# Eight modulation blocks instead of ten ahead of the first GEMM, each in a buffer of its own and loaded by one DMA

## Chip, cores and metric

The kernel runs on one core of one Trainium2 chip. The metric is the device time of one execution in microseconds (us), the median over several runs. One execution was also recorded by the hardware profiler; all rows below come from it. The engines are TensorE (PE for matmuls, PEld for weight loads), VectorE (DVE), ScalarE (ACT), GpSimd (POOL) and SyncE (SP), which issues the large DMAs.

## What is computed

Two transformer-like blocks follow each other on 256 latent tokens of width 1024; the first block also carries 256 context tokens. Here only the start matters. Nine modulation vectors per layer come from the conditioning vectors `c` and `c_ctx`, and shift, scale and gate what follows:

```python
def modulate(x, gain, shift, scale):
    return rms_norm(x, gain) * (1 + scale) + shift

def swiglu(h, w_in, w_out):
    a, b = jnp.split(h @ w_in, 2, axis=-1)
    return (jax.nn.silu(a) * b) @ w_out
# w_mod: (2 layers, 1024, 9 * 1024), applied to silu(c) and silu(c_ctx); b_mod is added
```

The first thing that the first block does is a SwiGLU on the modulated norm of x, which needs the shift and the scale of the first norm of layer 0, that is the first 2 × 1024 columns of `w_mod`.

## The kernel before

**Modulation blocks.** `w_mod` is taken in 72 blocks of 256 columns and 1024 rows (1 MB each, two tiles of 128 columns). A block goes through four engines. SP loads it as f32 (`mod_load`, L476 to L483): two DMAs of 512 KB, one for each tile, into `M32[k]`, where k alternates between two buffers. A tile's run in HBM is 128 floats, 512 bytes. ACT writes the f16 high part `MWH[k]` (`mod_split`, L954, in the helper `copy`, L944). DVE writes the f16 rest `MWL[k]` (`mod_split`, L1316, its instruction is L1319). PE multiplies both parts with silu(c) (`pe_mod`, L560, its matmuls are L568 and L569), and DVE drains the eight columns (`mod_drain`, L1321, L1325).

**What holds the blocks back.** SP may load a tile again when DVE has split the one before in that buffer (`mod_lo`). ACT may split a block when PE has used the one two before (`mod_used`). PE may start a block when the one two before is drained (`mod_drained`).

**The order at the start.** SP issues x and ctx, small rows, then the loads of the ten blocks of `MOD_FIRST`, then the first pair of weight blocks of the GEMM `ffn_0a_in` (four DMAs into `W32`, L487), then two modulation loads for that GEMM, then in a loop weights and modulation loads by turns. Each engine is one queue in program order, SP too. DVE splits a pair of blocks and then drains the pair before. After the tenth block come `mod_finish`, which adds the bias and makes the norm's gain, a small matmul for the relative bias (L749, L1574), three of four weight splits (L1313), and `dve_apply` of norm 0 (L1469, L1475) with ACT's half of it (L1060). Only then do both engines split the GEMM's first modulation blocks (`begin_mods`). On PE, block 0 of `ffn_0a_in` (`one`, L612, matmuls L608 to L610) starts chunk by chunk as norm 0 is applied. After it comes one modulation block, after weight block 1 another, and so on (`turn_of`, L646).

**POOL.** When the ten early blocks are used (`mod_used`, L1734), POOL issues the mask and 32 small-run loads `in_na_rpb` (L1743), and when they have landed it multiplies and adds on them (L1746, L1749). The result is used from the fourth GEMM on.

**The arena.** One SBUF tensor, `arena`, holds most of this at hand-set offsets: `M32` from 19968 on, `MWH` and `MWL` from 24064 on. Norm 0's squares take 0 to 4096, and `onehot` and `rel_mask` 8704 to 9728.

Of the kernel before, what the change touches and what calls it, by code (L numbers as in the profile page):

```python
# [21 lines left out]
ALU = mybir.AluOpType  # L22
# [4 lines left out]
P = 128  # L27
D = 1024
DC = D // P
# [16 lines left out]
W_SCALE = 64.0  # L46
# [85 lines left out]
def program(nc, io, out):  # L132
    ctx = ExitStack()
    with ctx:
# [3 lines left out]
        def sem(name):  # L138
            return ctx.enter_context(nc.semaphore(name))
# [46 lines left out]
        GH, GL = area(0, FC, BOTH, dt=F16), area(FC * SEQ, FC, BOTH, dt=F16)  # L186
        ffn_s, ffn_g = area(2 * FC * SEQ, 2, BOTH), area(2 * FC * SEQ + 1024, 2, BOTH)

        M32 = [area(19968 + 2048 * k, 2, DC, P) for k in range(2)]
        MWH = [area(24064 + 2048 * k, 2, DC, P, dt=F16) for k in range(2)]  # L190
        MWL = [area(25088 + 2048 * k, 2, DC, P, dt=F16) for k in range(2)]

# [36 lines left out]


        loaded = [[sem(f"loaded_{k}{t}") for t in range(2)] for k in range(2)]
        mod_loaded = [[sem(f"mod_loaded_{k}{t}") for t in range(2)] for k in range(2)]
        mod_hi, mod_lo = sem("mod_hi"), sem("mod_lo")
        mod_used, mod_drained = sem("mod_used"), sem("mod_drained")
        hi_ready = sem("hi_ready")
# [136 lines left out]


        MOD_BLOCKS = N_MOD * DC
        MOD_FIRST = 10
        m = MOD_FIRST
        for name, pairs in (("ffn_0a_in", FC // 2), ("ffn_0b_in", FC // 2), ("ffn_1a_in", 9)):
            g = next(x for x in GEMMS if x["name"] == name)
            g["mods"], g["m0"] = pairs, m
# [87 lines left out]
        @block.sync  # L467
        def _(sp):
            sp.dma_start(x_tok[0], io["x"][0].rearrange("(t p) d -> p t d", p=P)).then_inc(x_loaded, 16)
            sp.dma_start(x_tok[1], io["ctx"][0].rearrange("(t p) d -> p t d", p=P)).then_inc(x_loaded, 16)  # L470
            sp.wait_ge(rows_clear, 1)
            load_rows(sp, ROWS[:8])

            mod_w = io["w_mod"].rearrange("l (c p) n -> p l c n", p=P)

            def mod_load(m0, i, k):  # L476

                layer, first = divmod(m0, MOD_BLOCKS // 2)
                for t in range(2):
                    if not (isinstance(i, int) and m0 + 2 * i < 2):  # L480
                        sp.wait_ge(mod_lo, 2 * (m0 + k - 2) + t + 1 + 4 * i)
                    src = mod_w[:, layer, :, bass.ds(256 * (first + k) + P * t + 512 * i, P)]
                    sp.dma_start(M32[k][:, t], src).then_inc(mod_loaded[k][t], 16)  # L483

            def load(g, wv, k, t, col0, kp):
                src = wv[:, kp * g["kc"]:(kp + 1) * g["kc"], bass.ds(col0, P)]
                sp.dma_start(W32[:, k, t, 0:g["kc"], :], src).then_inc(loaded[k][t], 16)  # L487

            for g in GEMMS:
                wv = g["w"].rearrange("(c p) n -> p c n", p=P)  # L490

                def pair(i, slot_free, g=g, wv=wv):
                    for k in range(2):
                        for t in range(2):
                            slot_free(k, t)
                            if g["kind"] == "ffn":
                                load(g, wv, k, t, (2 * i + k) * P + t * FF, 0)
                            elif g["cols"] == 256:
                                load(g, wv, k, t, 512 * i + 256 * k + P * t, 0)
                            else:  # L500
                                load(g, wv, k, t, g["cols"][2 * i + k] + P * t, 0)

                def split_before(i, w0=g["w0"]):

                    return lambda k, t: sp.wait_ge(lo_ready, 2 * (w0 - 2 + k) + t + 1 + 4 * i)

                n, mods = g["blocks"] // 2, g["mods"]
                begin = 0
                if g["w0"] == 0:
                    for i in range(2):  # L510
                        for k in range(2):
                            mod_load(0, i, k)
                    with sp.Fori(2, MOD_FIRST // 2) as i:
                        for k in range(2):
                            mod_load(0, i, k)
                    pair(0, lambda k, t: None)
                    for k in range(2):
                        mod_load(g["m0"], 0, k)
                    begin = 1
                if mods:  # L520
                    if g["name"] == "ffn_0b_in":
                        pair(0, split_before(0))
                        sp.wait_ge(hy_lo, 4)
                        for k in range(2):
                            mod_load(g["m0"], 0, k)
                        begin = 1
# [12 lines left out]
                if g["parts"] == 2:  # L539
                    with sp.Fori(0, n // 2) as i:  # L540
                        for kp in range(2):
                            for k in range(2):
                                for t in range(2):
                                    split_before(2 * i + kp)(k, t)
                                    load(g, wv, k, t, 512 * i + 256 * k + P * t, kp)
                elif isinstance(g["cols"], list):
                    for i in range(n):
                        pair(i, split_before(i))
                elif begin < n:
                    with sp.Fori(begin, n) as i:  # L550
                        pair(i, split_before(i))

            sp.wait_ge(stored, 32)
# [3 lines left out]
        def _(pe):  # L557
# [43 lines left out]
            def pe_gemm(g, between={}):  # L601
# [44 lines left out]
                def turn_of(i, mods, first=False):  # L646
                    for b in range(2 * g["parts"]):
                        pair, kp = b // g["parts"], b % g["parts"]
                        one(b % 2, kp, pair, g["w0"] + b + 2 * g["parts"] * i, g["u0"] + pair + 2 * i, first and b == 0)
                        if mods:  # L650
                            pe_mod(g["m0"] + b + 2 * i, b)

# [289 lines left out]
        def _(act):  # L942
            def copy(dst, src, scale=1.0):
                return act.activation(dst, src, ACT.Copy, scale=scale)  # L944
# [6 lines left out]
                    act.wait_ge(loaded[k][t], 16 * (g["w0"] // 2 + 1) + 16 * i)  # L951
                    copy(WH[:, k, t, 0:g["kc"], :], W32[:, k, t, 0:g["kc"], :], W_SCALE).then_inc(hi_ready, 1)

            def mod_split(m0, i, k, first=False):  # L954

                if not first:
                    act.wait_ge(mod_used, m0 + k - 1 + 2 * i)
                for t in range(2):
                    act.wait_ge(mod_loaded[k][t], 16 * (m0 // 2 + 1) + 16 * i)
                    copy(MWH[k][:, t], M32[k][:, t], W_SCALE).then_inc(mod_hi, 1)  # L960

            def begin(g, ks=(0, 1)):
                for k in ks:
                    split(g, 0, k, True)

            def begin_mods(g):
                if g["mods"]:
                    for k in range(2):
                        mod_split(g["m0"], 0, k)
# [130 lines left out]
                act.activation(silu_c[:, :, s], pcol[:, at:at + DC], ACT.Silu).then_inc(silu_c_ready, 1)  # L1100
            act.wait_ge(silu_c_ready, 2)
            copy(silu_s[:, :, 0:2], silu_c[:, :, :]).then_inc(silu_hi, 1)
            for k in range(2):
                mod_split(0, 0, k, True)
            act_root(0)

            act.wait_ge(lg_abs, 1)
            act.activation(lgt[:, 1, :], lgt[:, 0, :], ACT.Exp, scale=-1.0).then_inc(lg_exp, 1)
            act.wait_ge(lg_u, 1)
            act.activation(lgt[:, 3, :], lgt[:, 2, :], ACT.Ln).then_inc(lg_ln, 1)  # L1110
            for i in range(1, MOD_FIRST // 2):
                for k in range(2):
                    mod_split(0, i, k)
            begin(GEMMS[0])

            def filter_step(n):
# [176 lines left out]
        def _(dve):  # L1293
# [15 lines left out]
            def split(g, i, k, tiles=(0, 1)):  # L1309

                for t in tiles:
                    dve.wait_ge(hi_ready, 2 * (g["w0"] + k) + t + 1 + 4 * i)
                    stt(WL[:, k, t, 0:g["kc"], :], W32[:, k, t, 0:g["kc"], :], W_SCALE, WH[:, k, t, 0:g["kc"], :],  # L1313
                        ALU.mult, ALU.subtract).then_inc(lo_ready, 1)

            def mod_split(m0, i, k):  # L1316
                for t in range(2):
                    dve.wait_ge(mod_hi, 2 * (m0 + k) + t + 1 + 4 * i)
                    stt(MWL[k][:, t], M32[k][:, t], W_SCALE, MWH[k][:, t], ALU.mult, ALU.subtract).then_inc(mod_lo, 1)  # L1319

            def mod_drain(m0, i, k):  # L1321

# [24 lines left out]
                link(ins)  # L1347

            def begin_mods(g):
                if g["mods"]:  # L1350
                    for k in range(2):
                        mod_split(g["m0"], 0, k)

# [194 lines left out]
            dve.wait_ge(silu_hi, 1)  # L1548
            tt(silu_s[:, :, 2:4], silu_c[:, :, :], silu_s[:, :, 0:2], ALU.subtract).then_inc(silu_s_ready, 1)
            dve_inverse(0)  # L1550
            for k in range(2):
                mod_split(0, 0, k)

            dve.wait_ge(lg_loaded, 32)
            stt(lgt[:, 0, :], lg[:, :], -1.0, lg[:, :], ALU.mult, ALU.max).then_inc(lg_abs, 1)
# [10 lines left out]
            for i in range(MOD_FIRST // 2):  # L1566
                if i + 1 < MOD_FIRST // 2:
                    for k in range(2):
                        mod_split(0, i + 1, k)
                for k in range(2):  # L1570
                    mod_drain(0, i, k)
            mod_finish(0, MOD_FIRST, [(0, 0)], [], [])
# [261 lines left out]
```

## Time and profile before

| | us |
|---|---|
| median of 3 runs | 2709.05 (2706.67 to 2709.97) |
| span of the profiled execution | 2703.6 |
| PE matmuls busy | 2579.7 (95%) |
| DVE busy | 1359.1 (50%) |
| ACT busy | 1091.2 (40%) |
| POOL busy | 247.2 (9%) |

The times are those of whole executions, and the span is that of one execution's instructions. Starts in the rows are microseconds from the start of the span. A row's "idle before" names what the engine waited for last. A row of a helper line (L944) says by its tile names what it works on.

### The profile page before, as it was taken

How to read it: one execution, taken by the hardware profiler on the slowest of the kernel's cores; microseconds unless marked ns; L12 is line 12 of the kernel's file. 1: busy time of each engine (PE TensorE's matmuls, PEld its weight loads, DVE VectorE, ACT ScalarE, POOL GpSimd, SP SyncE). 2: the span in 40 equal slices, each digit the busy share in tenths (PEclk: the TensorE clock that was granted, in tenths of full speed). 3: DMA queues.
4: the chain of work that ended last, by engine and by line, in shares of the span. 5: the costliest groups of instructions: out<-in, count | busy, mean ns of one | idle time of the engine just before them, and what ended most of it. 6: DMA issues, size and time to landing. Idle time of an engine off the chain costs nothing.

```text
span 2703.6 us, 45490 instructions
## 1 busy us (share of the span) xinstructions
PE 2579.7 (95%) x17855; PEld 1695.6 (63%) x17855; DVE 1359.1 (50%) x1911; ACT 1091.2 (40%) x1610; POOL 247.2 (9%) x235
## 2 busy tenths in 40 slices
PE   3899999999999999999999899999999999999999
PEld 3444444455644444444444578788888878778888
DVE  5855443363465553365432543466655545255654
ACT  5544323243354442254333311445544443344553
POOL 1800001004010000100002100120010000010001
PEclk7999999999999999999999999999999998589999
DMA  8976632330066653366543332258756754044674
GB/s 236 235 196 187 173 94 71 94 94 1 16 173 186 187 166 106 108 179 186 162 143 96 96 105 81 79 147 235 217 162 200 217 147 125 1 125 138 173 213 129
DMA packets 732733, 383.74 MB, mean 142 GB/s; under 512 B 12059, under 2 KB 729216, under 8 KB 732488
## 3 DMA queue, kind: packets, MB, share of 16 engines
q1 hardware_dynamic: 728312, 369.27, 48.7%
q0 software_dynamic: 3728, 10.98, 1.7%
q8 instruction: 85, 1.39, 0.2%
q10 hardware_dynamic: 576, 1.83, 0.2%
q14 instruction: 32, 0.26, 0.0%
HBM read 380.96 MB, written 1.08 MB: 141 GB/s over the span
## 4 chain that ended last, share of the span: by engine, by line
PE 88%; DVE 5%; DMA 3%; ACT 2%; issue 1%; POOL 0%; SPq 0%; ACTq 0%; DVEq 0%; POOLq 0%
PE PS L608 23%; PE PS L610 23%; PE PS L609 23%; PE PS L691 2%; DMA arena<-in_w_mod 2%; PE PS L627 2%; PE PS L626 2%; PE PS L625 2%; PE PS L715 2%; PE PS L694 1%; DVE WL L1313 1%; PE PS L863 1%; PE PS L585 1%; DVE arena L1469 1%; ACT WH L944 1%; PE PS L705 1%
## 5 line engine op out<-in xcount | busy, mean ns | idle before, releaser
L608 PE MATMUL PS<-XH,WH 128*128 128x256 f16 (+1 forms) x2912 | 948.5, 326 | 34.6 <-DVE XL L1475 20.8
L609 PE MATMUL PS<-XL,WH 128*128 128x256 f16 (+1 forms) x2912 | 948.0, 326 | 0.0
L610 PE MATMUL PS<-XH,WL 128*128 128x256 f16 (+1 forms) x2912 | 947.7, 325 | 0.0
L944 ACT ACTIVATE WH<-W 128x1024 f16<-128x1024 f32 (+1 forms) x520 | 550.4, 1106 | 636.8 <-PE PS L610 519.0
L1313 DVE SCALAR_TENSOR_TENSOR WL<-W,WH 128x1024 f16<-128x1024 f32 (+1 forms) x520 | 664.8, 1318 | 276.0 <-ACT WH L944 276.0
L608 PEld LDWEIGHTS PS<-XH,WH 128*128 128x128 f16 x2912 | 287.7, 99 | 222.9 <-issue 35.4
L610 PEld LDWEIGHTS PS<-XH,WL 128*128 128x128 f16 x2912 | 288.2, 99 | 181.7 <-issue 4.6
L608 PE MATMUL PS<-arena,WH 128*128 128x256 f16 (+1 forms) x1248 | 396.4, 318 | 1.9 <-DVE WL L1313 1.9
L609 PE MATMUL PS<-arena,WH 128*128 128x256 f16 (+1 forms) x1248 | 396.4, 318 | 0.0
L610 PE MATMUL PS<-arena,WL 128*128 128x256 f16 (+1 forms) x1248 | 396.4, 318 | 0.0
L609 PEld LDWEIGHTS PS<-XL,WH 128*128 128x128 f16 x2912 | 288.1, 99 | 171.9 <-issue 4.0
L976 ACT ACTIVATE arena<-PS 128x512 f32<-128x512 f32 (+1 forms) x132 | 64.6, 489 | 552.7 <-PE PS L610 552.7
L1359 DVE SCALAR_TENSOR_TENSOR arena<-PS,arena 128x512 f32<-128x512 f32 (+1 forms) x132 | 73.6, 558 | 401.7 <-ACT arena L976 401.7
L944 ACT ACTIVATE arena<-arena 128x1024 f16<-128x1024 f32 (+4 forms) x300 | 216.3, 761 | 50.4 <-DMA arena<-in_w_mod 20.7
L1720 POOL TENSOR_TENSOR arena<-arena 128x256 f32<-128x256 f32 (+1 forms) x60 | 80.0, 1334 | 1367.3 <-ACT arena L1020 1363.4
L1319 DVE SCALAR_TENSOR_TENSOR arena<-arena 128x1024 f16<-128x1024 f32 x144 | 173.1, 1243 | 21.9 <-ACT arena L944 21.8
L608 PEld LDWEIGHTS PS<-arena,WH 128*128 128x128 f16 x1248 | 122.1, 98 | 74.2 <-issue 4.5
L610 PEld LDWEIGHTS PS<-arena,WL 128*128 128x128 f16 x1248 | 122.1, 98 | 70.5
L609 PEld LDWEIGHTS PS<-arena,WH 128*128 128x128 f16 x1248 | 122.1, 98 | 70.0 <-issue 0.3
L1374 DVE TENSOR_SCALAR arena<-PS 128x512 f32<-128x512 f32 (+2 forms) x52 | 48.7, 937 | 190.0 <-PE PS L610 116.6
L944 ACT ACTIVATE arena<-PS 128x256 f32<-128x256 f32 (+1 forms) x117 | 49.4, 435 | 164.7 <-PE PS L705 95.1
L1428 DVE SCALAR_TENSOR_TENSOR X<-PS,modT,X 128x256 f32<-128x256 f32 x80 | 34.1, 479 | 154.5 <-PE PS L610 154.5
(225 smaller groups left out, 2309.1 us busy)
## 6 DMA issues: line engine op xcount, KB each, us to landing
arena<-in_w_mod SPq DMA_DIRECT2D x144, 512.0 KB, 6.8
W<-in_ffn_a_in SPq DMA_DIRECT2D x88, 512.0 KB, 5.0
W<-in_ffn_b_in SPq DMA_DIRECT2D x88, 512.0 KB, 4.7
W<-in_w_ffn_gu SPq DMA_DIRECT2D x88, 512.0 KB, 4.1
W<-in_ret_in SPq DMA_DIRECT2D x48, 512.0 KB, 4.1
W<-in_ffn_a_out SPq DMA_DIRECT2D x32, 704.0 KB, 5.5
W<-in_ffn_b_out SPq DMA_DIRECT2D x32, 704.0 KB, 5.9
W<-in_w_ffn_down SPq DMA_DIRECT2D x32, 704.0 KB, 5.7
```

The source lines that it names most:

```text
L608: mm(dst, wh, xh, start=(kp == 0 and c == 0), stop=False, skip_group_check=True)
L609: mm(dst, wh, xl, start=False, stop=False, skip_group_check=True)
L610: return mm(dst, wl, xh, start=False, stop=(kp == g["parts"] - 1 and c == kc - 1), skip_group_check=True)
L625: mm(dst, xh, wh, start=(c == 0), stop=False)
L626: mm(dst, xh, wl, start=False, stop=False)
L627: ins = mm(dst, xl, wh, start=False, stop=(c == kc - 1))
L944: return act.activation(dst, src, ACT.Copy, scale=scale)
L976: act.activation(ffn_s[:, k, 0:T], PS[:, 2 * k, 0:T], ACT.Silu, scale=1.0 / W_SCALE).then_inc(silu_done, 1)
L1313: stt(WL[:, k, t, 0:g["kc"], :], W32[:, k, t, 0:g["kc"], :], W_SCALE, WH[:, k, t, 0:g["kc"], :], ALU.mult, ALU.subtract).then_inc(lo_ready, 1)
L1319: stt(MWL[k][:, t], M32[k][:, t], W_SCALE, MWH[k][:, t], ALU.mult, ALU.subtract).then_inc(mod_lo, 1)
L1359: stt(ffn_g[:, k, 0:T], PS[:, 2 * k + 1, 0:T], 1.0 / W_SCALE, ffn_s[:, k, 0:T], ALU.mult, ALU.mult)\
L1720: tt(N["sq"][:, 0, 0:N["T"]], N["sq"][:, 0, 0:N["T"]], N["sq"][:, c, 0:N["T"]], ALU.add).then_inc(added_up, 1)
```

## The change

Ahead of the first GEMM there are eight modulation blocks instead of ten. Each has a buffer of its own, `M32_first[m]`: six areas of the arena not used by then, and the two of `M32`. SP issues the eight loads without a wait, one DMA of 1 MB each, whose runs in HBM are 256 floats, 1 KB. Blocks 8 and 9 move into `ffn_0a_in`: PE takes them after its weight block 0 and before its own block 10. SP loads them after the first weight pair. ACT and DVE split them at the head of `begin_mods`, and DVE drains each ahead of the split of block 10 or 11. All later modulation loads are also one DMA with one wait for both tiles. ACT and DVE read a tile as `M32[k][:, :, P * t:P * t + P]`, eight runs of 128 floats.

```diff
-        M32 = [area(19968 + 2048 * k, 2, DC, P) for k in range(2)]
+        M32 = [area(19968 + 2048 * k, DC, 2 * P) for k in range(2)]
+        M32_first = [area(n, DC, 2 * P) for n in (4096, 6144, 9728, 11776, 13824, 15872)] + M32
...
-        MOD_FIRST = 10
-        m = MOD_FIRST
+        MOD_FIRST, MOD_EARLY = 8, 2
+        m = MOD_FIRST + MOD_EARLY
...
-                for t in range(2):
-                    if not (isinstance(i, int) and m0 + 2 * i < 2):
-                        sp.wait_ge(mod_lo, 2 * (m0 + k - 2) + t + 1 + 4 * i)
-                    src = mod_w[:, layer, :, bass.ds(256 * (first + k) + P * t + 512 * i, P)]
-                    sp.dma_start(M32[k][:, t], src).then_inc(mod_loaded[k][t], 16)
+                sp.wait_ge(mod_lo, 2 * (m0 + k - 2) + 2 + 4 * i)
+                src = mod_w[:, layer, :, bass.ds(256 * (first + k) + 512 * i, 2 * P)]
+                sp.dma_start(M32[k], src).then_inc(mod_loaded[k], 16)
...
-                    for i in range(2):
-                        for k in range(2):
-                            mod_load(0, i, k)
-                    with sp.Fori(2, MOD_FIRST // 2) as i:
-                        for k in range(2):
-                            mod_load(0, i, k)
+                    for m in range(MOD_FIRST):
+                        sp.dma_start(M32_first[m], mod_w[:, 0, :, 256 * m:256 * m + 256]).then_inc(mod_first_loaded[m], 16)
                     pair(0, lambda k, t: None)
+                    for k in range(2):
+                        mod_load(MOD_FIRST, 0, k)
                     for k in range(2):
                         mod_load(g["m0"], 0, k)
...
                         one(b % 2, kp, pair, g["w0"] + b + 2 * g["parts"] * i, g["u0"] + pair + 2 * i, first and b == 0)
+                        if first and b == 0 and g["w0"] == 0:
+                            for m in range(MOD_FIRST, MOD_FIRST + MOD_EARLY):
+                                pe_mod(m, m % 2)
                         if mods:
                             pe_mod(g["m0"] + b + 2 * i, b)
...
+            def mod_first_split(m):
+                if m >= 2:
+                    act.wait_ge(mod_used, m - 1)
+                act.wait_ge(mod_first_loaded[m], 16)
                 for t in range(2):
-                    act.wait_ge(mod_loaded[k][t], 16 * (m0 // 2 + 1) + 16 * i)
-                    copy(MWH[k][:, t], M32[k][:, t], W_SCALE).then_inc(mod_hi, 1)
+                    copy(MWH[m % 2][:, t], M32_first[m][:, :, P * t:P * t + P], W_SCALE).then_inc(mod_hi, 1)
...
             def begin_mods(g):
-                if g["mods"]:
+                if g["w0"] == 0:
+                    for k in range(2):
+                        mod_split(MOD_FIRST, 0, k)
+                    for k in range(2):
+                        mod_drain(MOD_FIRST, 0, k)
+                        mod_split(g["m0"], 0, k)
+                elif g["mods"]:
                     for k in range(2):
                         mod_split(g["m0"], 0, k)
```

## Rows read from the trace of the kernel before

**Rows 1.** Chain that ended last, 0 to 160 us: start, length, what

```profile
1.25 10.52 DMA XL<-in_ctx
...
31.23 6.21 DMA arena<-in_w_mod
...
68.21 27.58 DMA arena<-in_w_mod
...
98.68 1.22 DVE WL L1313
99.95 0.39 PE PS L608
```

**Rows 2.** Timeline of DVE, 20 to 125 us: start, length, instruction, count, idle before

```profile
26.64 4.56 DVE L1319 SCALAR_TENSOR_TENSOR arena<-arena 128x1024 f16<-128x1024 f32 x4
...
34.02 2.36 DVE L1319 SCALAR_TENSOR_TENSOR arena<-arena 128x1024 f16<-128x1024 f32 x2 [0.29 <-ACT arena L944]
...
39.69 0.23 DVE L1325 TENSOR_REDUCE modT<-PS 128x4 f32<-128x8 f32 x2
42.11 3.60 DVE L1319 SCALAR_TENSOR_TENSOR arena<-arena 128x1024 f16<-128x1024 f32 x3 [2.19 <-ACT arena L944]
...
47.14 0.23 DVE L1325 TENSOR_REDUCE modT<-PS 128x4 f32<-128x8 f32 x2
...
55.43 0.23 DVE L1325 TENSOR_REDUCE modT<-PS 128x4 f32<-128x8 f32 x2
...
63.50 0.23 DVE L1325 TENSOR_REDUCE modT<-PS 128x4 f32<-128x8 f32 x2
```

**Rows 3.** Timeline of ACT, the same stretch

```profile
41.02 2.00 ACT L944 ACTIVATE arena<-arena 128x1024 f16<-128x1024 f32 x2 [2.50 <-PE PS L569]
```

**Rows 4.** DVE's timeline, then its group at 96 to 140 us: busy, mean ns

```profile
85.72 3.50 DVE L1319 SCALAR_TENSOR_TENSOR arena<-arena 128x1024 f16<-128x1024 f32 x3 [0.33 <-ACT arena L944]
...
L1319 DVE SCALAR_TENSOR_TENSOR arena<-arena 128x1024 f16<-128x1024 f32 x10 | 15.4, 1565 | 10.7 <-ACT arena L944 10.7
```

**Rows 5.** Timeline of PE, 60 to 125 us

```profile
74.15 0.59 PE L608 MATMUL PS<-XH,WH 128*128 128x512 f16 x1 [6.69 <-DVE XL L1475]
...
87.25 0.17 PE L568 MATMUL PS<-silu_s,arena 128*128 128x4 f16 x1
...
88.13 0.18 PE L568 MATMUL PS<-silu_s,arena 128*128 128x4 f16 x1 [0.34 <-DVE arena L1319]
...
88.55 0.38 PE L608 MATMUL PS<-XH,WH 128*128 128x512 f16 x1
```

**Rows 6.** Stretches: length, busy PE, PEld, DVE, ACT, POOL; PEclk; DMA share, GB/s

```profile
25.00:26.00 1.00, 0.73 (x7) 0.54 (x5) 0.23 (x1) 0.98 (x2) 0.00 (x0) 1.00 0.00 0
...
30.00:31.00 1.00, 0.55 (x16) 0.47 (x16) 1.00 (x2) 0.00 (x0) 0.00 (x0) 0.79 1.10 329
...
78.00:79.00 1.00, 1.00 (x5) 0.39 (x4) 1.00 (x1) 0.09 (x1) 1.00 (x3) 0.82 1.18 166
```

**Rows 7.** Page section 6 (us to landing), POOL's timeline, and stretches as in rows 6

```profile
W<-in_even_in SPq DMA_DIRECT2D x24, 512.0 KB, 3.9
...
66.50 19.45 POOL L1743 DMA_DIRECT2D arena<-in_na_rpb  x32
95.67 19.89 POOL L1746 TENSOR_TENSOR arena<-arena 128x256 f32<-128x256 f32 x16 [9.71 <-DMA arena<-in_na_rpb]
...
5.00:8.00 3.00, 0.00 (x0) 0.00 (x0) 0.00 (x0) 1.12 (x1) 3.00 (x7) 1.00 0.99 374
40.00:50.00 10.00, 3.68 (x128) 3.54 (x128) 5.40 (x7) 5.57 (x6) 0.00 (x0) 0.50 0.94 263
```

**Rows 8.** Waits of PE, 100 to 640 us, the longest: total, times, longest

```profile
PE PS L804 <- ACT arena L1163: 2.7, 1, 2.7
```

**Rows 9.** One line's durations (min/median/max ns); a group at 68 to 100 us

```profile
L1594 DVE SCALAR_TENSOR_TENSOR arena<-arena,pcol x12: 736/744/1015, 540.9 to 574.9; 128x510 f32<-128x510 f32 x12
...
L1475 DVE SCALAR_TENSOR_TENSOR XL<-arena,modT,XH 128x256 f16<-128x256 f32 x16 | 7.3, 467 | 0.0
```

More of the change, by code:

```diff
@@ L231, in program @@
         loaded = [[sem(f"loaded_{k}{t}") for t in range(2)] for k in range(2)]
-        mod_loaded = [[sem(f"mod_loaded_{k}{t}") for t in range(2)] for k in range(2)]
+        mod_loaded = [sem(f"mod_loaded_{k}") for k in range(2)]
+        mod_first_loaded = [sem(f"mod_first_loaded_{m}") for m in range(8)]
         mod_hi, mod_lo = sem("mod_hi"), sem("mod_lo")
@@ L952, in split, with mod_split @@
                     copy(WH[:, k, t, 0:g["kc"], :], W32[:, k, t, 0:g["kc"], :], W_SCALE).then_inc(hi_ready, 1)
-            def mod_split(m0, i, k, first=False):
-                if not first:
-                    act.wait_ge(mod_used, m0 + k - 1 + 2 * i)
+            def mod_first_split(m):
+                if m >= 2:
+                    act.wait_ge(mod_used, m - 1)
+                act.wait_ge(mod_first_loaded[m], 16)
                 for t in range(2):
-                    act.wait_ge(mod_loaded[k][t], 16 * (m0 // 2 + 1) + 16 * i)
-                    copy(MWH[k][:, t], M32[k][:, t], W_SCALE).then_inc(mod_hi, 1)
+                    copy(MWH[m % 2][:, t], M32_first[m][:, :, P * t:P * t + P], W_SCALE).then_inc(mod_hi, 1)
+            def mod_split(m0, i, k):
+                act.wait_ge(mod_used, m0 + k - 1 + 2 * i)
+                act.wait_ge(mod_loaded[k], 16 * ((m0 - MOD_FIRST) // 2 + 1) + 16 * i)
+                for t in range(2):
+                    copy(MWH[k][:, t], M32[k][:, :, P * t:P * t + P], W_SCALE).then_inc(mod_hi, 1)
             def begin(g, ks=(0, 1)):
@@ L1102, in _ @@
             copy(silu_s[:, :, 0:2], silu_c[:, :, :]).then_inc(silu_hi, 1)
-            for k in range(2):
-                mod_split(0, 0, k, True)
+            for m in range(2):
+                mod_first_split(m)
             act_root(0)
@@ L1110, in _ @@
             act.activation(lgt[:, 3, :], lgt[:, 2, :], ACT.Ln).then_inc(lg_ln, 1)
-            for i in range(1, MOD_FIRST // 2):
-                for k in range(2):
-                    mod_split(0, i, k)
+            for m in range(2, MOD_FIRST):
+                mod_first_split(m)
             begin(GEMMS[0])
@@ L1314, in split, with mod_first_split @@
                         ALU.mult, ALU.subtract).then_inc(lo_ready, 1)
+            def mod_first_split(m):
+                for t in range(2):
+                    dve.wait_ge(mod_hi, 2 * m + t + 1)
+                    stt(MWL[m % 2][:, t], M32_first[m][:, :, P * t:P * t + P], W_SCALE, MWH[m % 2][:, t],
+                        ALU.mult, ALU.subtract).then_inc(mod_lo, 1)
             def mod_split(m0, i, k):
@@ L1318, in mod_split @@
                     dve.wait_ge(mod_hi, 2 * (m0 + k) + t + 1 + 4 * i)
-                    stt(MWL[k][:, t], M32[k][:, t], W_SCALE, MWH[k][:, t], ALU.mult, ALU.subtract).then_inc(mod_lo, 1)
+                    stt(MWL[k][:, t], M32[k][:, :, P * t:P * t + P], W_SCALE, MWH[k][:, t], ALU.mult, ALU.subtract).then_inc(mod_lo, 1)
             def mod_drain(m0, i, k):
@@ L1349, in begin_mods @@
             def begin_mods(g):
-                if g["mods"]:
+                if g["w0"] == 0:
+                    for k in range(2):
+                        mod_split(MOD_FIRST, 0, k)
+                    for k in range(2):
+                        mod_drain(MOD_FIRST, 0, k)
+                        mod_split(g["m0"], 0, k)
+                elif g["mods"]:
                     for k in range(2):
@@ L1550, in _ @@
             dve_inverse(0)
-            for k in range(2):
-                mod_split(0, 0, k)
+            for m in range(2):
+                mod_first_split(m)
             dve.wait_ge(lg_loaded, 32)
@@ L1568, in _ @@
                     for k in range(2):
-                        mod_split(0, i + 1, k)
+                        mod_first_split(2 * i + 2 + k)
                 for k in range(2):
```

## The prediction

> **What bounds the kernel now.** I read the page first. TensorE (PE) is busy for 95% of the span, and its own chain ends last for 88% of it. A change ahead of the first GEMM can therefore move the time only through the moment from which PE runs without a break. The page gives `arena<-in_w_mod` 2% of the chain, and the chain in order of time shows all of it inside the first 96 us: four waits for modulation loads between 31 and 62 us, the first of which is shown, then one of 27.58 us, and from 99.95 us only PE [rows 1]. The waits of PE from 100 to 640 us name none for weights or modulation blocks [rows 8]. The kernel splits into three stages. Up to 63.5 us modulation pairs go around a ring of loads, splits and drains [rows 2]. Up to 87.25 us norm 0 is applied, and the first weight block of `ffn_0a_in` runs with it. From 88.55 us PE has its second block [rows 5]. The number wanted is how far this last start moves. The profiled execution has a span of 2703.6 us, 5.45 us under the median of 2709.05. I add the move to both.
>
> **The pair removed ahead of the GEMM, and the loads no longer in its way.** DVE's drains of two blocks at a time stand at 39.69, 47.14, 55.43 and 63.50 us: pairs of 7.45, 8.29 and 8.07 us [rows 2]. Two things make up a pair. One is PE's turn and ACT's first split: drain at 39.69, ACT at 41.02 [rows 3], first DVE split at 42.11, so 2.42 us. The other is four DVE splits, at best 4.56 us when all data is there (26.64 us), some 4.7 us when ACT paces them (3.60 for three, 2.36 for two) [rows 2]. That is 7.12 us without DMA waits. With every block in a buffer of its own SP queues all eight loads from the start. 8.4 MB behind x and ctx, which have landed at 11.8 us [rows 1], land by about 44 us at the 263 GB/s of the 512 B runs [rows 7], and the first weight pair by 52, always ahead of ACT, which would reach block 6 at 47 and the weights at 51. The first split at 26.64 stays, as it waits for norm 0's sums and not for a load. The second pair starts at 34.02 as now, and its drain comes at 34.02 + 4.7 = 38.72. The next two follow at 45.84 and 52.96. This third drain is the last one, which now stands at 63.50: **10.54 us earlier**, of which 8.07 are the removed pair and 2.47 DMA waits. If the rings keep the fastest pair seen (7.45) it is 9.9.
>
> **What follows unchanged.** From the last drain to the end of block 0 the same instructions stand on the same engines, the weight splits, the apply and block 0, bound by DVE and without a modulation load among them. Block 0 ends at 87.25 − 10.54 = 76.71 us. TensorE's clock is at its lower level (0.50) there and rises at 78 us, 4 us after block 0 starts [rows 5, 6]. I take this to move along, since the clock is low before it in either kernel.
>
> **The two blocks moved into the GEMM, and the new wait.** After block 0 PE must now take blocks 8 and 9, then block 10 (the first of the GEMM's own), and only then weight block 1, in this order. Blocks 8 and 10 share buffer M32[0]. So block 10's load cannot start before DVE has split block 8, and DVE does this only after the apply. In the kernel before, block 10 was long in its buffer at that point, and PE lost only 88.55 − 87.25 = 1.30 us between the blocks [rows 5]. Now, step by step:
> - DVE's two splits of block 8 stand where those of block 10 stand now: from 85.72, two of three splits that take 3.50, so until 88.05 [rows 4], just before PE's use at 88.13 [rows 5]. Minus 10.54 that is 77.5 us. DVE goes on to block 9 and is done at 79.9.
> - SP wakes and issues block 10's load: 0.1 us, from the kernel's own step between such a split and its load [rows 1, 2]. Block 11's load waits for block 9's split (79.9). The weight loads of pair 1 are queued on SP behind both of them and so start after 80 us instead of 70.5. They are needed at 99 us and have the DMA rings to themselves by then, so nothing waits.
> - The landing of 1 MB is nowhere in the trace alone. 512 KB loads in a quiet stretch take 3.9 us [rows 7]. The second half adds 1.1 us at the 374 GB/s at which 4 KB runs moved at 5 to 8 us, or 2.0 us at 263 [rows 7]: 5.0 to 5.9 us. Beside it lies the tail of `in_na_rpb`: 32 loads on POOL's queue, released by the last early block, so issued until about 75.4 us instead of 85.95 [rows 7]. They landed up to 9.7 us after the last issue ended [rows 7], which would be 85.1 here. One load of SP's beside them took 27.58 us [rows 1]. I take 6.9 us, near the quiet row, because most of the POOL queue is gone when the load starts, with ends of 5.0 and 9.4. Landing: 84.5 us.
> - ACT splits tile 0 in 1.06 us, DVE both tiles in 2 × 1.2 us (1.57 each if POOL's bias work runs beside them [rows 4]), PE takes the second tile in 0.42 us (88.13 to 88.55 [rows 5]). Block 1 starts at 84.5 + 1.1 + 2.5 (with the hops) + 0.45 = 88.6 us. Now it starts at 88.55: **the head start of 10.5 us is eaten by a wait of 10.5 us.**
> - The clock. PE's dense work ended at 25.7 us, and at 30.8 us the clock fell, though bursts of modulation matmuls ran in between. After a start it took 4.1 us to rise [rows 6]. Here 11.9 us lie between block 0 and block 1, with only such bursts, so block 1 starts at 1.2 GHz: ten matmuls of 0.427 us in 4.2 us [rows 5, 6] instead of 2.16. **Cost 2.1 us**, with nothing to cover it. If the clock stays up, 0.
> - The wait of 0.2 us ahead of block 2 (DVE's weight split ended at 99.90, delayed by block 11's late landing [rows 1, 5]) goes: −0.15.
>
> Sum: −10.54 + 10.6 + 2.06 − 0.15 ≈ **+2.0 us**: span 2705.6, median **2711.0 us**.
>
> The Trainium skill, "DMA: Bandwidth & Descriptors", Specifications, names 512 B as the smallest transfer at line rate, so 1 KB runs would bring nothing. This trace does not agree: 512 B runs moved 263 GB/s at a DMA share of 0.94, runs of 4 KB 374 at 0.99 [rows 7]. The same page (Anatomy of one DMA, a fit for the path from GpSimd) has 2.0 us plus bytes over 436 GB/s, an estimate of 4.4 us for block 10. The sum by it would be −0.5 us.
>
> **Edits at nothing.** One wait and one load per block in place of two in the later GEMMs: PE waits for none of them now [rows 8] and has a whole turn of 22 us for each; without that cover it would be one split, 1.2 us. ACT and DVE read each tile in eight pieces instead of one: the count of elements is the same. DVE's L1594, whose operands lie in two pieces, took 744 ns for 510 elements, where 256 take 467 and 1024 take 1170, which makes 700 on a straight line [rows 4, 9]. That 6% on the twelve splits of the ring is the upper bound, 0.9 us, and 0 the lower. I take 0, as one of two pieces is also shifted by an element there. POOL's bias work moves earlier by about 13 us, beside DVE's splits, as it is now; its users come hundreds of microseconds later.
>
> **Rivals.**
> (a) **The load of block 10 is caught by the `in_na_rpb` loads.** For: a load of 512 KB issued at 68.21 landed at 95.81, together with the last of them, at 95.67 [rows 1, 7]. Against: that one was issued 2 us after their start, this one some 2 us after their end. It decides from a landing time of 10.3 us (6.9 + 3.4). At 14 us the kernel is 9 us slower, 2718. Chance 0.17 for above 10.3.
> (b) **The head start survives.** If the wait for block 10 were short, say because block 8 is split before the apply ends, block 1 would start near 80 us and the time would be 2701. Against it stand the order of DVE's program and the shared buffer. With the quickest landing, no fall of the clock and no POOL beside it the sum is only −1.9 − 2.1 + 2.0 = −2.0 us. Chance 0.06.
> (c) **The change does not relieve the ring**: the pairs stay as long as they are, because the splits pace them. Then 8.07 instead of 10.54 is gained and the time is 2713.5. It counts within the forecast, since it stays below the bound.
>
> **How the numbers follow.** Forecast, the two cancel: 0.77. A measurement of this kernel can tell about 0.2%, 5.4 us, from no change. Low end: landing 5.0 (−1.9), clock not falling (−2.1) and the forecast's +2.0 give −2.0, so 2707, and 2706 with the runs' own spread. High end: landing 9.4 (+2.5), POOL beside the splits (+0.7), tiles read in pieces (+0.9), pairs of 7.45 (+0.6) and the forecast's +2.0 give +6.7, so 2715.8; half of (a) takes it to 2718. Faster 0.06, same 0.77, slower 0.17.
>
> **What would show it.** Drains at about 38.7, 45.8 and 53.0; block 0 ending near 76.7; PE idle from 80.4 to about 86 with DMA `in_w_mod` as the last cause; block 1 starting at 88 to 90 with matmuls of 0.43 us; all later starts moved by one constant. It is wrong if block 10's landing is far from 6.9 us, if ACT finds a block missing before 51 us, or if block 2 waits for its weights.

## The result and the profile after

The changed kernel takes 2712.38 us (median of 15 runs, 2708.07 to 2717.31) against 2707.26 us for the kernel before on the same chip (15 runs). The ratio is 1.0018, with a 95% interval from 1.0011 to 1.0026: slower by 5.1 us (3.0 to 7.0), where 2.0 us were forecast. The span of its profiled execution is 2707.0 us, 3.4 us above the one before.

DVE's timeline shows the early ring (start, length, instruction, count, idle before), as in [rows 2]:

```profile
34.89 4.63 DVE L1328 SCALAR_TENSOR_TENSOR arena<-arena 128x1024 f16<-128x1024 f32 x4 [0.30 <-ACT arena L945]
39.44 0.23 DVE L1340 TENSOR_REDUCE modT<-PS 128x4 f32<-128x8 f32 x2
41.86 4.63 DVE L1328 SCALAR_TENSOR_TENSOR arena<-arena 128x1024 f16<-128x1024 f32 x4 [2.19 <-ACT arena L945]
46.41 0.23 DVE L1340 TENSOR_REDUCE modT<-PS 128x4 f32<-128x8 f32 x2
...
53.38 0.23 DVE L1340 TENSOR_REDUCE modT<-PS 128x4 f32<-128x8 f32 x2
```

The drains (L1340) now come every 6.97 us, and no DMA stands among what DVE waited for. The chain that ended last shows what follows the apply, then PE's timeline the same from PE's side, to be read beside [rows 1, 5]:

```profile
75.60 2.37 DVE arena L1334 x2
77.99 12.92 DMA arena<-in_w_mod
91.00 1.07 ACT arena L945
92.08 2.98 DVE arena L1334 x2
```

```profile
77.14 0.17 PE L566 MATMUL PS<-silu_s,arena 128*128 128x4 f16 x1
...
93.45 0.18 PE L566 MATMUL PS<-silu_s,arena 128*128 128x4 f16 x1 [12.60 <-DVE arena L1334]
...
95.56 0.59 PE L606 MATMUL PS<-XH,WH 128*128 128x512 f16 x1
```

Block 0 ends at 77.14 us, 10.1 us earlier than before. Block 1 starts at 95.56, 7.0 us later: the load of block 10 took 12.92 us from issue to landing, and PE stood for 12.60 us in one piece. The stretches (length, then busy PE, PEld, DVE, ACT and POOL, granted clock, DMA share, GB/s) show the rings and the clock:

```profile
76.00:81.00 5.00, 3.34 (x71) 2.33 (x68) 4.31 (x5) 2.41 (x3) 0.00 (x0) 1.00 0.96 73
81.00:91.00 10.00, 0.00 (x0) 0.00 (x0) 0.00 (x0) 0.01 (x1) 2.83 (x5) 0.53 0.84 233
```

From 76 to 81 us the DMA engines were busy at a share of 0.96 and moved 73 GB/s. POOL's timeline names what they did (as in [rows 7]):

```profile
56.38 19.50 POOL L1764 DMA_DIRECT2D arena<-in_na_rpb  x32
88.17 17.40 POOL L1767 TENSOR_TENSOR arena<-arena 128x256 f32<-128x256 f32 x16 [12.29 <-DMA arena<-in_na_rpb]
```

The last of the small-run loads landed 12.3 us after the last issue ended, and block 10 only after it.

### The profile page after: what moved, and what is told of

Its sections match the earlier page's. It is cut to its first block, busy times and chain, and to the rows that moved or that the text cites. A ratio compares the mean times of both kernels' runs of the same rounds, so it can differ in the third digit from the quotient of the medians.

```text
span 2707.0 us, 45210 instructions
## 1 busy us (share of the span) xinstructions
PE 2574.6 (95%) x17855; PEld 1693.0 (63%) x17855; DVE 1356.9 (50%) x1911; ACT 1089.7 (40%) x1610; POOL 241.9 (9%) x235
## 4 chain that ended last, share of the span: by engine, by line
PE 89%; DVE 7%; ACT 2%; DMA 1%; issue 1%; POOL 0%; ACTq 0%; SPq 0%; POOLq 0%; DVEq 0%
PE PS L606 23%; PE PS L607 23%; PE PS L608 23%; PE PS L692 2%; PE PS L625 2%; PE PS L624 2%; PE PS L623 2%; PE PS L716 2%; DVE WL L1322 1%; PE PS L695 1%; DVE arena L1490 1%; PE PS L864 1%; DVE XL L1496 1%; PE PS L583 1%; PE PS L566 1%; PE PS L706 1%
## 5 line engine op out<-in xcount | busy, mean ns | idle before, releaser
L606 PEld LDWEIGHTS PS<-arena,WH 128*128 128x128 f16 x1248 | 122.1, 98 | 74.1 <-issue 4.5
L1334 DVE SCALAR_TENSOR_TENSOR arena<-arena 128x1024 f16<-128x1024 f32 x128 | 154.0, 1246 | 16.0 <-ACT arena L945 16.0
```

Source lines behind the costliest of these rows:

```text
L606: mm(dst, wh, xh, start=(kp == 0 and c == 0), stop=False, skip_group_check=True)
L1334: stt(MWL[k][:, t], M32[k][:, :, P * t:P * t + P], W_SCALE, MWH[k][:, t], ALU.mult, ALU.subtract).then_inc(mod_lo, 1)
```

## The experiments

Each was timed beside the kernel before on the same chip. The runs stood on different chips, so two of them are compared by their ratios. "Inverse" is the start of DVE's inverse of norm 0 (the reciprocal in its timeline), which stands just ahead of the first split of a modulation block. "Block 1" and "block 2" are the starts of the first GEMM's second and third weight block in PE's timeline. All starts are in us, each from one profiled execution.

| kernel | ratio to before (95%) | inverse | block 1 | block 2 |
|---|---|---|---|---|
| before | 1 | 25.77 | 88.55 | 99.95 |
| changed | 1.0018 (1.0011 to 1.0026) | 26.64 | 95.56 | 108.29 |
| e1_na_late | 1.0024 (1.0014 to 1.0035) | 27.73 | 88.14 | 100.75 |
| e2_own_10_11 | 0.9977 (0.9968 to 0.9986) | 24.68 | 81.11 | 94.92 |
| e3_ten_own | 0.9978 (0.9969 to 0.9987) | 25.92 | 84.68 | 95.84 |
| e4_filler | 1.0014 (1.0004 to 1.0023) | 25.81 | 94.57 | 107.42 |
| e5_two_dmas | 1.0020 (1.0011 to 1.0029) | 24.88 | 93.57 | 106.33 |
| f1_paced | 0.9988 (0.9979 to 0.9997) | 26.07 | 86.51 | 100.20 |
| f2_order | 0.9999 (0.9990 to 1.0008) | 25.43 | 79.53 | 98.91 |
| f3_own_order | 0.9960 (0.9948 to 0.9973) | 26.82 | 80.89 | 92.85 |
| f4_own_order_paced | 0.9959 (0.9946 to 0.9973) | 25.66 | 79.73 | 91.69 |
| f5_before_paced | 0.9992 (0.9983 to 1.0001) | 25.48 | 90.08 | 101.25 |

The inverse lies anywhere from 24.68 to 27.73 us, so a start says something of a kernel only with the inverse of its row taken off. One source is the landing of x and ctx, for which PE's first matmul waits: it started at 11.90 and 11.81 us in the two executions with the old early loads, and at 11.39 to 13.70 us in the ten with the new ones. Whether the new loads add something to that wait is open.

The old early stage itself is not the same in two executions. `f5_before_paced` differs from the kernel before only in what POOL does after the tenth block, and yet two of its rings took over 9 us (DVE's timeline, to be read beside [rows 2]):

```profile
39.33 0.23 DVE L1325 TENSOR_REDUCE modT<-PS 128x4 f32<-128x8 f32 x2
48.61 0.23 DVE L1325 TENSOR_REDUCE modT<-PS 128x4 f32<-128x8 f32 x2
55.86 0.23 DVE L1325 TENSOR_REDUCE modT<-PS 128x4 f32<-128x8 f32 x2
65.03 0.23 DVE L1325 TENSOR_REDUCE modT<-PS 128x4 f32<-128x8 f32 x2
```

From the inverse to the fourth drain that is 39.55 us, against 37.73 in [rows 2]. With buffers of their own the rings took 6.96 to 6.98 us in all ten executions. The DMA waits that the new buffers remove were thus worth 1.8 us more in the one execution than in the other.

**The small-run loads released later.**

```diff
-            pool.wait_ge(mod_used, MOD_FIRST)
+            pool.wait_ge(mod_used, 16)
             pool.dma_start(na_mask, io["k_na_mask"]).then_inc(nab_loaded, 16)
```

> One part beside the change: POOL's 32 small-run loads and their mask are released by modulation block 16 instead of block 8, so that nothing but SP's own queue is on the DMA rings when block 10 is loaded. All else is the changed kernel. Theory (the load of block 10 was caught behind the tail of these loads, 12.9 us from issue to landing): it lands in 5 to 6 us, block 1 of the first GEMM starts near 88.5 us instead of 95.7, and the kernel is about 7 us faster than the changed one, within 2 us of the kernel before. Rival (a 1 MB load of 1 KB runs takes that long by itself, or waits for SP's own backlog): landing stays at 12 to 13 us and the time with it, 5 us above the kernel before.

The landing and block 1 came as the theory has them, and the time did not: 1.0024. Two pieces of its chain:

```profile
79.08 5.02 DMA arena<-in_w_mod
```

```profile
149.70 30.47 DMA arena<-in_w_mod
```

The burst, issued from 146.57 us on, now lay beside the load of block 18, which took 30.47 us. (The expectation below, which speaks of blocks 14 and 15, counted wrong: SP issues the loads in pairs, and the fifth pair from block 10 on is the one at 149.70.) PE waited for it, with the clock falling again (its timeline):

```profile
182.83 0.17 PE L566 MATMUL PS<-silu_s,arena 128*128 128x4 f16 x1 [4.08 <-DVE arena L1334]
...
184.43 0.19 PE L566 MATMUL PS<-silu_s,arena 128*128 128x4 f16 x1 [1.04 <-DVE arena L1334]
...
186.16 0.61 PE L606 MATMUL PS<-XH,WH 128*128 128x512 f16 x1 [1.15 <-DVE WL L1322]
```

So the cause of the long landing is shown: without the burst the same load took 5.02 us. But moving the burst only moves the victim. The next run spreads it.

**The same loads in eight groups of four.**

```diff
-            pool.wait_ge(mod_used, MOD_FIRST)
+            pool.wait_ge(mod_used, 12)
...
             for h in range(NA_HEADS):
+                pool.wait_ge(mod_used, 12 + 2 * h)
```

> The changed kernel with POOL's small-run loads neither beside block 10's load nor in one burst: four of the 32 are released by each second modulation block from block 12 on. Theory (a burst of these loads holds any load of SP's that lies beside it for some 13 to 28 us; in the run where they were only released later, at 146 us, it was the loads of blocks 14 and 15, and PE lost 7.8 us there): block 10 lands in 5 to 6 us, block 1 starts at the time of the kernel before, no later wait comes, and the kernel is 0 to 2 us slower than the kernel before, which is the price of the fallen clock. Rival (later loads wait for a reason of their own): PE waits at 170 to 190 us again and the time stays at 2712 to 2714.

Its chain shows the load alone, and PE's waits from 100 us on name no modulation load:

```profile
77.43 5.04 DMA arena<-in_w_mod
```

Block 1 started at 86.51 us and the ratio is 0.9988, 3 us better than the kernel before, where 0 to 2 us worse were expected. The mechanism is confirmed, since nothing but the burst differs from the changed kernel and 8 us are gone. That it ends below the kernel before is explained only in part. From the inverse to block 2 it takes 74.1 us, as the profiled execution of the kernel before does (74.2), but `f5_before_paced`, the old kernel with the same spread loads, takes 75.8.

**The shared buffer.**

```diff
+        M32_late = [area(n, DC, 2 * P) for n in (13824, 6656)]
...
-                sp.wait_ge(mod_lo, 2 * (m0 + k - 2) + 2 + 4 * i)
+                if m0 == MOD_FIRST + MOD_EARLY and isinstance(i, int) and i == 0:
+                    sp.wait_ge(mod_lo, 16)
+                else:
+                    sp.wait_ge(mod_lo, 2 * (m0 + k - 2) + 2 + 4 * i)
```

> One part beside the change: blocks 10 and 11, the GEMM's first own ones, get buffers of their own (13824 and 6656 of the arena) and are loaded right after blocks 8 and 9, so that their loads no longer wait for the splits after the apply. Theory (the shared buffer makes the wait between block 0 and block 1): block 1 starts when DVE has split blocks 8, 9 and 10, near 83.5 us instead of 95.7, the clock still falls (at about 82 us, cost 1.5 to 2 us), and the kernel is 3 to 4 us faster than the kernel before. Rival (the queue on SP and the small-run loads of POOL hold any load of that time): block 10 lands after 85 us all the same and the time stays above the kernel before.

2700.19 us. By the ratios this is 6 us under the kernel before, where 3 to 4 were expected, and 11 under the changed one. With the small-run loads where they were, the wait for the load is gone from the chain. DVE paces PE instead (rows of the chain, then two stretches):

```profile
73.63 4.63 DVE arena L1345 x4
78.26 0.08 DVE modT L1351
78.33 2.28 DVE arena L1345 x2
```

```profile
80.00:82.00 2.00, 1.44 (x23) 0.80 (x21) 0.68 (x2) 0.00 (x0) 0.00 (x0) 0.50 0.98 143
...
84.00:86.00 2.00, 2.00 (x6) 0.76 (x5) 0.49 (x1) 1.58 (x2) 1.55 (x3) 0.50 0.75 224
```

The clock had still fallen, as expected, and block 1 ran at 0.43 us a matmul until 86.4 us: 13.81 us from block 1 to block 2, where 48 matmuls of 0.216 and one modulation block take 11.2.

**The own buffers alone, with all ten blocks ahead.**

```diff
-        MOD_FIRST, MOD_EARLY = 8, 2
+        MOD_FIRST, MOD_EARLY = 10, 0
...
-        M32_first = [area(n, DC, 2 * P) for n in (4096, 6144, 9728, 11776, 13824, 15872)] + M32
+        M32_first = [area(n, DC, 2 * P) for n in (4096, 6144, 9728, 11776, 13824, 15872, 17920)]
+        M32_first += [XH[:, :, :].rearrange("p c t -> p (c t)").bitcast(F32).rearrange("p (c n) -> p c n", c=DC)] + M32
```

> One part of the change alone: all ten blocks stay ahead of the GEMM, each in a buffer of its own with one load of 1 KB runs (17920 of the arena and the space of XH are added); none is moved into the GEMM. Theory (the own buffers take the DMA waits out of the ring, and only the move of two blocks makes the new wait): drains every 6.97 us, the last pair's at 60.4 us instead of 63.5, block 1 starts about 3.2 us earlier than in the kernel before, with no fall of the clock between the blocks, and the kernel is 3 us faster than the kernel before, ratio 0.999. Rival (ring gain is given back because POOL's loads and the weight loads now collide elsewhere): block 2 or later waits and the time is that of the kernel before.

The edit also makes SP wait, ahead of the load into the space of XH and those after it, until PE has turned x and ctx (`x_turned`). Result: 2701.22 us, ratio 0.9978, which is 6 us faster where 3 were expected. The fourth drain in its DVE timeline stands 3.87 us ahead of the one in [rows 2]:

```profile
59.63 0.23 DVE L1338 TENSOR_REDUCE modT<-PS 128x4 f32<-128x8 f32 x2
```

This one pair of executions does not account for 6 us. Counted from the inverse, the drain comes 4.0 us earlier than in [rows 2] and 5.8 us earlier than in `f5_before_paced`. The early part of the change is a gain by itself. The move of two blocks into the GEMM, as it was built, with block 10 in the buffer of block 8, turned it into a loss.

**PE's order.**

```diff
                         if mods and first and g["w0"] == 0:
+                            if b == 1:
+                                for k in range(2):
+                                    pe_mod(g["m0"] + k, k)
+                        elif mods:
                             pe_mod(g["m0"] + b + 2 * i, b)
```

> The changed kernel with PE's order changed: block 10 is taken after weight block 1, ahead of block 11, and no longer before it; buffers, loads and POOL are those of the changed kernel. Theory (PE's own order turns the late load into a wait of 15 us): block 1 starts right after blocks 8 and 9, near 81 us instead of 95.7, with no fall of the clock, and the rest of the late loads shows ahead of block 2, which starts near 98 instead of 108 us; the time is within 2 us of the kernel before. Rival (the loads themselves are the bound): block 2 starts after 104 us and the time stays 4 us above.

> Both remedies: blocks 10 and 11 in buffers of their own (that run was 6 us under the kernel before) and block 10 after weight block 1 in PE's order. Theory: block 1 starts after blocks 8 and 9 without a fall of the clock, which saves a further 2.4 us of wait and 2.8 us of slow matmuls, partly taken back ahead of block 2 by DVE's queue: 3 to 4 us under that run, near 2696 to 2697 us, ratio 0.996. Rival (DVE is the bound of this stage either way): no gain over that run.

The first came out as expected in time and starts: block 1 at 79.53 us, block 2 at 98.91, ratio 0.9999, although the load of block 10 was as late as ever (its chain):

```profile
76.79 12.71 DMA arena<-in_w_mod
```

The order does not remove the wait for that load; it puts a whole weight block in front of it. The expectation on the clock missed. The gap from block 0 to block 1 was 3.60 us, filled with modulation matmuls and without a pause over 0.6 us, and the clock had still fallen, near 78.2 us. Block 1 began with some twelve matmuls of 0.43 us:

```profile
78.00:80.00 2.00, 1.43 (x34) 1.07 (x35) 1.10 (x2) 0.00 (x0) 0.00 (x0) 0.55 0.98 35
```

The second, with the own buffers, took 2696.23 us, ratio 0.9960, as expected. In its execution the clock stayed up through a gap of the same length (3.58 us), to be read against the stretch above and against the one from 80 to 82 us in the run with own buffers only:

```profile
80.00:82.00 2.00, 1.53 (x22) 0.94 (x23) 2.00 (x4) 0.79 (x1) 0.00 (x0) 1.00 0.82 219
```

So a gap of 3.6 us did not settle whether the clock fell; it fell in one of these two executions. How much of this run's gain over the one with own buffers only (0.9960 against 0.9977) is clock and how much is order is open.

**All three remedies, and the burst in the kernel before.**

> The kernel with own buffers for blocks 10 and 11 and PE's new order (11 us under the kernel before) with POOL's small-run loads also spread, four by four from block 12 on. Theory (block 11's landing still holds DVE's queue ahead of weight block 2, and the small-run loads delay it): block 11 is there before ACT asks, DVE's weight splits end 2 to 3 us earlier, block 2 starts 1 to 1.5 us earlier, and the kernel is about 1 us under that run, 2695. Rival: DVE's queue alone sets block 2's start, and the time is the same.

> The kernel before with POOL's small-run loads spread in the same way and nothing else changed. Theory (in the kernel before the burst lies beside loads that PE needs only at 99 us, so it costs what the trace shows ahead of block 2, 0.2 us): within 1 us of the kernel before, ratio 1.000. Rival (the burst costs the kernel before as much as it costs the changed one): 3 us or more faster than the kernel before.

Spreading the loads adds nothing that can be told to the two remedies (0.9959 against 0.9960). The theory missed, and the rival's forecast of the time came true: from the inverse to block 2 both runs take 66.03 us. DVE's weight splits ahead of block 2 did end some 5 us earlier, counted from the inverse, but PE has no wait ahead of block 2 in either run, so nothing came of it. In the kernel before, spreading gives 0.9992, with an interval from 0.9983 to 1.0001, that is from 4.6 us faster to 0.3 us slower. The trace offers 0.2 us for it. Both the theory (within 1 us) and the rival (3 us or more) have values in the interval, so this stays undecided.

**The DMAs and the clock.**

```diff
-                sp.dma_start(M32[k], src).then_inc(mod_loaded[k], 16)
+                for t in range(2):
+                    sp.dma_start(M32[k][:, :, P * t:P * t + P], src[:, :, P * t:P * t + P]).then_inc(mod_loaded[k], 16)
```

> The one-DMA part undone: the changed kernel with two DMAs of 512 KB and runs of 512 B for each modulation block again, early and late, in the same buffers and with one wait for both. Theory (the early stage is paced by DVE's splits and PE never waits for the later loads, so run length only changes landings): the early drains stay at 6.97 us, block 10 lands 0 to 3 us later, and the kernel is 0 to 3 us slower than the changed one. Rival (the 1 KB runs carry the early gain): the ring slows to 7.4 us or more a pair and the time goes up by over 3 us.

The ring kept its 6.97 us (drains at 37.68 and 44.65 us). The second half of block 10 landed 12.03 us after its issue and 12.44 after that of the first half, which is no later than the 12.92 of the single load. The time is that of the changed kernel within the intervals, some 2.5 us either way: one DMA per block is worth nothing that can be told here.

```diff
                                 pe_mod(m, m % 2)
+                            for _ in range(56):
+                                mm(PS[:, 4, :], WH[:, 1, 0, 0, :], XH[:, 0, :], start=True, stop=True, skip_group_check=True)
```

> The clock's price alone: the changed kernel with 56 matmuls of 512 columns added on PE after blocks 8 and 9, into a bank that nothing reads (12.1 us at the higher clock level, as long as the wait for block 10). They compute nothing that is used. Theory (the clock falls in the wait, and block 1's first matmuls take 0.43 us): block 1 starts at the same 95.7 us but at the higher level, 1.5 us are saved, ratio to the kernel before 1.0013 in place of 1.0018. Rival (the clock does not matter to the sum): no change, or slower if the added matmuls outlast the wait.

This one does not answer its question. The added matmuls ended at 92.1 us, block 1 could start only at 94.57, and the clock fell near 95 us (a stretch of its trace), so the slow matmuls were paid all the same. That its ratio is the expected one, 1.0014, says nothing for the theory; it is as close to the changed kernel's 1.0018:

```profile
96.00:98.00 2.00, 2.00 (x6) 0.68 (x5) 2.00 (x3) 1.09 (x2) 2.00 (x3) 0.50 0.94 280
```

## Why the prediction was right, and which terms were off

**The direction and the frame held.** Both effects were there, they largely cancel, and the wait for block 10 is on the path for the reason given: a buffer freed only after the apply, and PE's fixed order. Own buffers (11 us by the ratios) and the order (5 us) each take it from between block 0 and block 1. The size was partly luck. The landing, the term on which the forecast named itself wrong if it came out far from 6.9 us, took 12.92. The forecast of the time, 2711.0, came within 1.4 us of 2712.38, but the shift was missed by 3.1: the base of 2709.05 from three runs stands 1.8 us above the later median of the kernel before.

**The ring.** Forecast 7.12 us a pair, measured 6.97. The executions start 0.87 us apart (DVE's inverse of norm 0 at 25.77 us before, 26.64 after). With that taken off, the drains stand at 38.57, 45.54 and 52.51, forecast 38.72, 45.84 and 52.96, and block 0 ends at 76.27, forecast 76.71. Reading tiles in eight pieces cost nothing: the first four splits, for which all data was there, took 4.56 us in either kernel. What the ring gained over the kernel before was sized from one execution, and by `f5_before_paced` it can be 1.8 us more.

**The landing of block 10 is the mis-sized term.** Taken 6.9 us with an upper end of 9.4, measured 12.92. The step that failed is "most of the POOL queue is gone when the load starts": 2.1 us after the last issue, when block 10's load was issued, the last of the small-run loads was still 10.2 us from landing. This is rival (a), which was given 0.17, and at a landing of 12.9 us it is past the 10.3 from which it was said to decide. By the forecast's own sum such a landing gives about 2717 us; that the measured time is 2712.38 does not speak for this term. The quiet bound of 5.0 was right to a tenth (5.02 and 5.04 us in the two runs without the burst). What misled me is that I sized the queue's tail from an execution in which SP's loads took nearly half of the engines' time. I took their absence for a quicker end; the end came 12.3 us after the last issue instead of 9.7. Their absence is not shown to be what lengthened it: in the run with the burst at 146 us SP's loads lay beside it, and the end came 12.15 us after the last issue.

**After the landing.** From landing (90.91) to block 1 it took 4.65 us instead of 4.05, as POOL's bias work ran beside DVE's two splits (2.98 us instead of 2.4), which the forecast had left in its upper end.

**The clock.** A mean of 0.84 over 81 to 82 us puts the fall near 81.7 us, 4.5 us after block 0's last matmul. [rows 6] read the same way (0.79 over 30 to 31 us) puts it near 30.6 and not 30.8 us, 4.8 us after the dense work. But the clock rose 3.2 us after block 1 began, not 4.1, and this is no constant: in the run with the burst at 146 us it took 3.1 us, in the spread run 5.2 and in the run with own buffers 5.4. The 0.6 us that it saved against the forecast lie within this spread. From block 1 to block 2 the changed kernel took 12.73 us and the kernel before 11.40, so 1.33 us net of the vanished wait of 0.2, where 1.9 was forecast.

Together: 2.0 forecast + 0.87 (start of the execution) − 0.5 (ring) + 6.0 (landing) + 0.6 (splits) − 0.6 (clock) = 8.4 us, and block 2 starts at 108.29 against 99.95, 8.34 later. **The span grew by 3.4 only.** The same 15156 matmuls, from the same one to the end, took less time (one stretch of before, then of after, columns as above):

```profile
441.54:2703.60 2262.06, 2186.80 (x15156) 1497.96 (x15154) 1126.56 (x1604) 908.85 (x1388) 167.42 (x138) 0.96 0.48 135
```

```profile
449.93:2707.00 2257.07, 2180.80 (x15156) 1495.77 (x15154) 1126.58 (x1604) 909.19 (x1388) 167.64 (x138) 0.96 0.47 135
```

PE's busy time in them differs by 6.0 us for the same matmuls. The granted clock of 120 equal slices of each stretch, added up, shows why: it was at the lower level for some 174 us in the first and 164 us in the second, and ten microseconds less at half the clock are 5 us. Other runs put this part at 2261.5 us (small-run loads spread), 2261.6 (own buffers) and 2259.4 (own buffers and order). From block 2 to the end the changed kernel took 2598.7 us and the kernel before 2603.7. With the changed kernel's buffers and order, `e5_two_dmas` took 2598.8 and `e4_filler` 2602.5, and `f2_order` took 2604.5, so the short end does not go with the change alone. One profiled pair is therefore no measure of a shift to within 5 us. The median over the runs (+5.1) lies between the 8.3 us at block 2 and the 3.4 us of the pair, and the interval reaches up to 7.0 us. Part of the distance from 8.3 to 5.1 can be named: 0.87 us are the start of the execution, and with `f5_before_paced` for the kernel before, whose rings took 1.8 us longer, block 2 comes 5.9 us later, counted from the inverse. Both are single executions, so this is an indication and no proof.

## What to carry to other kernels

A head start is worth what the first wait behind it leaves. Before work is moved past a queue point, list what its load waits for (a shared buffer, a split that comes after other work) and what stands behind it in the engine's order; here the fix was a buffer and the place of one block, not less work. A burst of loads with small runs that holds up a needed load is better spread than moved: moved, it only picked another victim (1.0024); spread, it left no wait for a load (0.9988). And a forecast sized from one profiled execution carries that execution's luck, here 1.8 us in a ring and 2 us in the rise of the clock.

## What was new about the hardware

A burst of 32 loads of 64 KB with 256 B runs on POOL's queue holds up a load of SP's until the burst has landed. Issued 2.1 us after the last of the 32, block 10's load took 12.92 us, against 5.02 without them; loads issued among them took 27.58 and 30.47 us. From 56 to 81 us in the changed kernel the queues' lines (packets, MB, share of 16 engines) are these:

```profile
q0 software_dynamic: 1066, 2.30, 88.1%
q1 hardware_dynamic: 928, 0.93, 13.1%
```

And from 81 to 88 us:

```profile
q1 hardware_dynamic: 1513, 1.53, 62.0%
q0 software_dynamic: 38, 0.06, 24.0%
```

The line q0 is POOL's queue and q1 SP's. So 2.3 MB took 22 us of all engines (88.1% of 25 us). In the kernel before the burst took 16 us of them (51.4% of 66 to 97 us), and beside SP's loads at 146 to 180 us 20 us (58.0%). It is no fixed cost, as I had expected, and what sets it is open.

The lines from 81 to 88 us show something that the landing alone hides. From 81 to 88 us SP's queue moved 1.53 MB, more than the whole of block 10, and block 10 still landed only at 90.91 us, after the last small-run load at 88.17. What held it at the end was therefore not the rate of SP's queue as a whole. Which of the 16 engines finished its share last, no view shows.

The Trainium skill, "DMA: Bandwidth & Descriptors", SWDGE vs HWDGE vs iDMA, says that an engine goes round its queues and changes only at packet boundaries. The rows neither bear this out nor speak against it. A packet of POOL's queue carries 2.2 KB (2.30 MB / 1066), one of SP's 1 KB, so strict turns would leave SP's queue a third of the bytes. Between 149.7 and 166 us in the run with the burst at 146 us, SP's queue got 3.5 packets through for each of POOL's:

```profile
q0 software_dynamic: 709, 1.45, 66.4%
q1 hardware_dynamic: 2505, 1.50, 32.1%
```

No run here takes the packets apart, so the mechanism stays open.

The run length matters where a queue is alone. In the run with the burst moved to 146 us, 79 to 92 us in 40 slices, first the modulation loads with 1 KB runs, then weights with 512 B runs:

```profile
GB/s 0 0 0 76 101 233 375 372 391 391 378 391 356 391 331 350 353 337 365 343 359 347 326 326 291 298 291 292 295 293 293 290 288 240 265 314 310 309 255 102
```

Some 390 GB/s against 290. These are loads of two different tensors. The changed kernel and the run with two DMAs per block compare the same loads into the same buffers, 24 to 34 us, 1 KB runs first and 512 B runs second (stretches as above):

```profile
24.00:34.00 10.00, 5.86 (x96) 5.32 (x94) 6.22 (x10) 7.26 (x10) 0.00 (x0) 0.82 1.10 348
```

```profile
24.00:34.00 10.00, 4.06 (x80) 3.56 (x78) 7.60 (x14) 7.35 (x10) 0.00 (x0) 0.73 1.19 291
```

That is 348 GB/s against 291, a fifth more. Run length and size of a DMA change together here. It is a rate that this kernel has no use for, since DVE's splits pace the stage.
